# Eight weight buffers in turn for the experts of a two-layer trunk

## The reference

```python
def moe_ffn(h, router_w, router_b, w_gate, w_up, w_down):
    ...
    _, idx = lax.top_k(sel, TOP_K)              # 2 of 16 experts for each token
    ...
    for e in range(N_EXPERTS):
        he = jax.nn.silu(t @ w_gate[e]) * (t @ w_up[e])
        out = out + gates[:, e:e + 1] * (he @ w_down[e])
```

## Time and profile before

| | us |
|---|---|
| three runs, median (lowest, highest) | 1375.0 (1374.42, 1381.2) |
| profiled execution, own time | 1374.44 |
| its span | 1372.6 |
| PE busy in the span | 1196.2 (87%) |
| DVE, ACT, POOL busy | 396.4, 221.3, 132.2 |
| moved by DMA | 325.45 MB, mean 237 GB/s |
| chain that ended last: PE, DMA, DVE | 79%, 10%, 6% |

### The profile page before, as it was taken

The page is one execution under the profiler, slowest core; times in us unless marked ns, Lnnn a source line. Parts: engine busy times, 40 slices in busy tenths (PEclk is TensorE's granted clock), DMA queues, the critical chain, the costliest instruction groups (busy, mean ns, idle before and its releaser), DMA issues.

```text
span 1372.6 us, 14516 instructions
## 1 busy us (share of the span) xinstructions
PE 1196.2 (87%) x5812; PEld 656.6 (48%) x5812; DVE 396.4 (29%) x742; ACT 221.3 (16%) x414; POOL 132.2 (10%) x118
## 2 busy tenths in 40 slices
PE   4899998899999399999999099989999399999772
PEld 1444444676644245454544055646764245545440
DVE  0131114774323712121201531126532501111002
ACT  2120121112312210101010312231121210011000
POOL 0002101630000000000000201112100000000001
PEclk8899998979999599999999599999999599999997
DMA  9321115443543269999997512236256269999994
GB/s 358 152 76 61 63 61 213 186 177 131 197 171 122 93 225 401 427 403 430 400 428 270 179 62 82 102 123 234 104 233 276 105 229 397 429 426 426 428 428 177
DMA packets 34016, 325.45 MB, mean 237 GB/s; under 512 B 5664, under 2 KB 5664, under 8 KB 16288
## 3 DMA queue, kind: packets, MB, share of 16 engines
q1 hardware_dynamic: 23328, 292.03, 52.9%
q0 software_dynamic: 4896, 17.83, 3.6%
q10 hardware_dynamic: 5728, 14.68, 2.8%
HBM read 308.79 MB, written 15.74 MB: 236 GB/s over the span
## 4 chain that ended last, share of the span: by engine, by line
PE 79%; DMA 10%; DVE 6%; ACT 2%; issue 2%; POOL 1%; SPq 0%; ACTq 0%; DVEq 0%; POOLq 0%
PE ps L781 14%; PE ps L1123 13%; PE ps L1120 8%; PE ps L1150 6%; PE ps L1025 6%; PE ps L768 6%; PE ps L1145 4%; DMA arena<-in_w_down 4%; PE ps L714 3%; PE ps L938 2%; DMA ring<-in_w_mod 2%; DMA arena<-in_w_up 2%; PE ps L954 2%; PE ps L1100 2%; PE ps L982 1%
## 5 line engine op out<-in xcount | busy, mean ns | idle before, releaser
L781 PE MATMUL ps<-ring,featT 128*128 128x512 f32 (+1 forms) x480 | 186.9, 550 | 0.0
L781 PEld LDWEIGHTS ps<-ring,featT 128*128 128x128 f32 x480 | 90.8, 190 | 92.3 <-issue 89.9
L1933 DVE TENSOR_TENSOR arena<-arena,ps 128x256 f32<-128x256 f32 (+1 forms) x32 | 16.7, 522 | 284.6 <-PE ps L1123 151.1
L1123 PE MATMUL ps<-ring,arena 128*128 128x512 f32 x192 | 90.1, 627 | 2.4 <-ACT arena L1407 2.4
L1123 PE MATMUL ps<-arena 128*128 128x512 f32 x192 | 84.9, 595 | 2.4 <-ACT arena L1407 2.4
L1150 PE MATMUL ps<-arena 128*128 128x512 f32 x192 | 85.3, 597 | 0.0
L768 PE MATMUL ps<-featT,ring 128*128 128x512 f32 (+1 forms) x192 | 82.6, 589 | 2.3 <-ACT featT L1231 2.3
L1145 PE MATMUL ps<-arena 128*64 128x512 f32 x320 | 74.3, 607 | 10.9 <-DMA arena<-in_w_down 6.6
L1025 PE MATMUL ps<-ring,featT 128*128 128x512 f32 x192 | 82.7, 592 | 0.0
L1120 PE MATMUL ps<-arena 128*64 128x256 f32 x640 | 75.1, 388 | 6.3 <-DMA arena<-in_w_up 3.8
L1120 PE MATMUL ps<-ring,arena 128*64 128x256 f32 x640 | 73.4, 382 | 4.6 <-DMA ring<-in_w_gate 2.3
(11 more groups left out here) (276 smaller groups left out, 1406.4 us busy)
## 6 DMA issues: line engine op xcount, KB each, us to landing
arena<-in_w_down SPq DMA_DIRECT2D x32, 2048.0 KB, 15.0
ring<-in_w_mod SPq DMA_DIRECT2D x21, 2048.0 KB, 7.5
arena<-in_w_gate SPq DMA_DIRECT2D x16, 2048.0 KB
arena<-in_w_up SPq DMA_DIRECT2D x16, 2048.0 KB, 14.6
ring<-in_w_gate SPq DMA_DIRECT2D x16, 2048.0 KB, 12.4
ring<-in_w_up SPq DMA_DIRECT2D x16, 2048.0 KB, 13.3
ring<-in_w_in SPq DMA_DIRECT2D x10, 2048.0 KB, 8.1
ring<-in_w_out SPq DMA_DIRECT2D x4, 2048.0 KB, 8.0
```

Source lines behind the costliest of these rows:

```text
L781: o = mm(bank[:, lo:hi], featT[:, k, P * i:P * i + P], W[:, k, lo:hi], start=k == 0, stop=k == KD - 1)
L1123: o = mm(ps[:, m, :], X_[:, k, :], W[:, k, :], start=k == 0, stop=k == KD - 1)
```

## The change

There are eight buffers of 2 MB: the six from before, `tokA` (called `rows`) and `featT`. The matrices of a layer are numbered in the order in which PE uses them, gate 0, up 0, (none), gate 1, up 1, down 0, gate 2, up 2, down 1, ..., and matrix n goes to buffer n % 8, but for three of each 24. A refill waits for the product that read that buffer's last matrix.

Ahead of the experts SP issues gate 0, up 0, gate 1, up 1 when attention is done, down 0 when the output projection is done, and, once the order is known, gate 2, up 2 (behind `turn_pe`) and down 1 (behind `f_stored`). Then come the refills: the first round's first half is written out, the rest is a loop of 24 matrices for each 8 experts. The last matrix, down 15, goes to `rows` behind gate 14. PE waits on the semaphore of the buffer. DVE counts `rows_free` at a round's end, after a wait for its own last sum into `h`.

```diff
+        rows = tokA.rearrange("p t d -> p (t d)")
+        buffers = [slots[2], slots[3], rows, slots[4], slots[5], ring[:, 0, :], ring[:, 1, :], featT.rearrange("p k c -> p (k c)")]
...
+        N_TURN = 24
+        def buffer_of(n):
+            return {8: 2, 9: 0, 10: 1}.get(n % N_TURN, n % 8)
+        def load_of_weights(p, j):
+            return 3 * p + j + (3 if j == 2 else 0)
+        def position(n):
+            return n // 3 - (n % 3 == 2), n % 3
+        def last_in_buffer(n):
+            return next(m for m in range(n - 1, -N_TURN, -1) if buffer_of(m) == buffer_of(n))
+        def loads_so_far(n):
+            return sum(buffer_of(m) == buffer_of(n) and m != 2 for m in range(n + 1))
...
                 sp.wait_ge(S("na_out"), upto("na_out", l, nt))
-                load_expert(0, 0, 2)
-                for j in range(3):
-                    load_expert(1, 1, j)
+                for n in (0, 1, 3, 4):
+                    load_expert(position(n)[0], n)
                 for n in range(N_OUT):
                     name, ll, value = use_of(("out", l, n))
                     sp.wait_ge(S(name), upto(name, ll, value))
-                load_expert(0, 0, 0)
-                load_expert(0, 0, 1)
+                load_expert(0, 5)
...
-                wide_weights(1, expert_at(2), 0)
-                with sp.Fori(0, more * (NE // 2) + (NE // 2 - 2)) as i:
-                    e = [expert_at(i * 2 + 2 + n) for n in range(3)]
-                    wide_weights(i * 2 + 2, e[1], 1)
-                    down_weights(i * 2 + 1, e[0], 0)
-                    wide_weights(i * 2 + 3, e[2], 0)
-                    down_weights(i * 2 + 2, e[1], 1)
-                ...
+                def load_behind(n, place, e):
+                    p, j = position(last_in_buffer(n))
+                    if buffers[buffer_of(n)] is rows and position(n) == (1, 2) and not isinstance(place, int):
+                        sp.wait_ge(S("rows_free"), first * 2 + i)
+                    sp.wait_ge(S(("gate_pe", "up_pe", "dn_pe")[j]), first * NE + place + (p + 1))
+                    load_expert(e, n)
+                e = {p: expert_at(p) for p in range(2, 4)}
+                load_expert(e[2], 6)
+                sp.wait_ge(S("turn_pe"), upto("turn_pe", l, KD))
+                load_expert(e[2], 7)
+                sp.wait_ge(S("f_stored"), upto("f_stored", l, 16))
+                load_expert(1, 8)
+                load_behind(9, 0, e[3])
+                load_behind(10, 0, e[3])
+                load_behind(11, 0, e[2])
+                for n in range(12, N_TURN, 3):
+                    ...
+                    load_behind(n, 0, now)
+                    load_behind(n + 1, 0, now)
+                    load_behind(n + 2, 0, behind)
+                with sp.Fori(1, R * 2) as i:
+                    for n in range(0, N_TURN, 3):
+                        ...
+                        load_behind(n, i * (N_TURN // 3), now)
+                        load_behind(n + 1, i * (N_TURN // 3), now)
+                        load_behind(n + 2, i * (N_TURN // 3), behind)
+                last = expert_at(NE - 1)
+                sp.wait_ge(S("gate_pe"), first * NE + more * NE + (NE - 1))
+                load_expert(last, 2)
...
-                    pe.wait_ge(S(f"slot{3 * (q % 2) + m}"), r.all * (NE // 2 * 16) + (q // 2 + 1) * 16)
-                    return slots[3 * (q % 2) + m].rearrange("p (k c) -> p k c", k=k)
+                    n = load_of_weights(q, m)
+                    b = buffer_of(n)
+                    per_round = 6
+                    pe.wait_ge(S(f"slot{b}"), r.all * (per_round * 16) + loads_so_far(n) * 16)
+                    return buffers[b].rearrange("p (k c) -> p k c", k=k)
...
+                if l == 0:
+                    dve.sem_inc(S("rows_free"), 1)
...
                     add_rows(n_round)
+                    dve.wait_ge(S("h_end"), NT + ended(l, first, n_round, T))
+                    dve.sem_inc(S("rows_free"), 2)
```

More of the change, by code:

```diff
@@ L623, in _, with load_expert @@
                         layer_rows(l)
-                def load_expert(e, c, j):
-                    slot = 3 * c + j
-                    src = (ins["w_gate"], ins["w_up"], ins["w_down"])[j]
+                def load_expert(e, n):
+                    src = (ins["w_gate"], ins["w_up"], ins["w_down"])[n % 3]
                     w = src[l, e] if isinstance(e, int) else src[l, bass.ds(e, 1)].rearrange("o p c -> (o p) c")
-                    sp.dma_start(slots[slot], w).then_inc(S(f"slot{slot}"), 16)
+                    b = buffer_of(n)
+                    sp.dma_start(buffers[b], w).then_inc(S(f"slot{b}"), 16)
                 sp.wait_ge(S("na_out"), upto("na_out", l, nt))
-                load_expert(0, 0, 2)
-                for j in range(3):
-                    load_expert(1, 1, j)
+                for n in (0, 1, 3, 4):
+                    load_expert(position(n)[0], n)
                 for n in range(N_OUT):
@@ L667, in _ @@
-                with sp.Fori(0, more * (NE // 2) + (NE // 2 - 2)) as i:
-                    e = [expert_at(i * 2 + 2 + n) for n in range(3)]
-                    wide_weights(i * 2 + 2, e[1], 1)
-                    down_weights(i * 2 + 1, e[0], 0)
-                    wide_weights(i * 2 + 3, e[2], 0)
-                    down_weights(i * 2 + 2, e[1], 1)
-                e = [expert_at(NE - 2), expert_at(NE - 1)]
-                wide_weights(more * NE + (NE - 2), e[1], 1)
-                down_weights(more * NE + (NE - 3), e[0], 0)
@@ L676, in _ @@
-                down_weights(more * NE + (NE - 2), e[1], 1)
+                def load_behind(n, place, e):
[5 more added lines that the diff above has]
+                e = {p: expert_at(p) for p in range(2, 4)}
@@ new lines, in _ @@
+                load_expert(e[2], 6)
[7 more added lines that the diff above has]
+                for n in range(12, N_TURN, 3):
+                    p = n // 3
+                    now, behind = expert_at(p), expert_at(p - 1)
+                    load_behind(n, 0, now)
+                    load_behind(n + 1, 0, now)
+                    load_behind(n + 2, 0, behind)
@@ new lines, in _ @@
+                with sp.Fori(1, R * 2) as i:
+                    for n in range(0, N_TURN, 3):
+                        p = i * (N_TURN // 3) + n // 3
+                        now, behind = expert_at(p), expert_at(p + (NE - 1))
+                        load_behind(n, i * (N_TURN // 3), now)
[3 more added lines that the diff above has]
+                sp.wait_ge(S("gate_pe"), first * NE + more * NE + (NE - 1))
```

## The result

| | before | after |
|---|---|---|
| median of 20 runs, us | 1375.5 | 1382.3 |
| lowest, highest | 1366.7, 1392.3 | 1377.7, 1395.5 |
| profiled execution, own time | 1374.44 | 1377.88 |
| its span | 1372.6 | 1376.0 |

The changed kernel is slower: ratio 1.0081, 95% interval 1.0058 to 1.0104. The ratio (+11 us) is wider than the step between the medians (+6.8 us) and than that between the means of all twenty executions (+6.4 us, 0.47%), because it leaves out the five longest executions of the kernel before (1389 to 1392 us) and none of the changed one, of which seven are as long (1388.6 to 1395.5).

A forecast was written before the change was run, and what follows sets the result against it. It took TensorE to bound layer 0's expert part and, late in layer 1's, the weight transfers. Terms +6.0 + 6.4 - 6.8 + 0.2 = +5.8 us on 1374.44 gave 1380.2, say 1380; range 1368 to 1386.

The forecast's parts named there:

- What bounds each layer: Expert parts: TensorE sets layer 0; in layer 1 transfers take over from 1250.80 us, with a ceiling of 21.6 us to win.
- The collision: Each layer's first gather of token rows meets the three early loads and lands later: +6.0 us in layer 0, +6.4 in layer 1.
- The step that took the median of the other gathers: First gather of each layer: expected to take 10.7 us, the median over all 22 gathers, instead of 4.70 and 4.32.
- Rival A: First gathers slip in between the loads and land at 6.4 us: -2.8 us in all, 1371.6; chance 0.25.
- rival B: First gathers wait for all three loads (+8, +9), layer 1 gives back only -2.2: +15.0 us, 1389; chance 0.25.
- The gain: Layer 1's expert part: prefetch less the pauses of the new buffer order, -6.8 us, bounds -9.8 and -2.8; layer 0: 0.
- The prefetch itself: Layer 1's expert part: two matrices fewer to move while the DMA engines are full, 9.8 us less; 0 in layer 0.
- the first pause: Layer 1: up 5's refill waits for g3's end, leaving the DMA engines dry up to 3.6 us, taken as +3.0.
- The second pause: Down 9's refill waits for d7, gate 11 and up 11 queued behind it: taken as 0, up to 4 us in layer 1.
- DVE's added wait: DVE's wait for its own last row sum, once per layer, before the next layer's statistics: +0.1 to +0.3 us, taken as 0.2.
- the step from the sum to the call: From +5.8 us and a 0.5% bound of 6.9 us to chances: faster 0.15, within 0.5% 0.52, slower 0.33.

The follow-up runs named there:

- e6: The e2 kernel, but in layer 0 the three extra matrices wait until gate product 0 is done: 1370.2 us, ratio 0.9989 to the kernel before.
- e3: The changed kernel with its eight buffers in plain first-in-first-out order: 1380.1 us, ratio 1.0042 to the kernel before.
- e7: The changed kernel timed again without an edit: 1379.5 us, ratio 1.0058 to the kernel before.
- e1: The changed kernel with gate 2, up 2 and down 1 issued only after the layer's first gather has landed: 1368.8 us, ratio 0.9953 to the kernel before.
- e2: The changed kernel with down 1 issued before the order is known, gate 2 with it, up 2 behind the first gather: 1367.0 us, ratio 0.9937 to the kernel before.
- e5: The changed kernel with the edits of e2 and e3 together: 1368.0 us, ratio 0.9959 to the kernel before.

## Why the prediction was right or wrong

Its time, 1380, lies between the profiled execution and the median, and its range holds both. Its call was wrong: it put 0.52 on a change within 0.5% and 0.33 on slower, and the ratio says slower.

**What bounds each layer: right.** Layer 0's 256.66 us don't move in any of the kernels, with five, six or eight matrices ahead (e6, before, after). In layer 1 the distance follows the transfers.

**The collision: right in place, cause and size.** Forecast +6.0 and +6.4, measured +6.6 and +6.3 from issue to landing. The step that took the median of the other gathers for the row to go by held. Rival A, in which the gather slips in between, is out. The rule on turns between queues (the Trainium skill, "DMA: Bandwidth & Descriptors", section "Queues, rings and completion order") isn't contradicted: the gather landed at 481.7, 2.3 us before the third matrix, which was issued at 465.96 and took 18.0. These runs don't show how long one turn is. (The +8 of rival B for layer 0 was worked out too high: by the prediction's own numbers the end of the three loads is +7.3.)

**The gain: mis-sized.** Forecast -6.8, measured 235.62 - 227.14 = 8.5. The prefetch itself is right: e3 gets 9.85 of the two matrices' 9.8. The term that was off is the first pause, set at 3.0: e3 says 1.4. The working had the engines without work for up to 3.6 us there. They weren't: in the 12 us around it (1166 to 1178 us) they are busy to 0.99 and move 374 GB/s, where the kernel before moves 411 (1154 to 1166). The missing 0.44 MB are 1.0 us. The second pause, set at 0, costs nothing that can be seen, by the rates given at e3.

**The rest.** DVE's added wait was set at 0.2: the next layer's statistics start 1.39 us behind the start of the last sum, where it was 1.15. The first two products of layer 1 took 15.56 us instead of 17.04. That is the clock's rise at the start of the experts, not the change: it is 15.4 to 17.1 over all runs, 17.06 in e7 of the same kernel, and the granted clock of the first 4 us is 0.60 here and 0.50 in e1, where the two take 16.95. Without this the profiled pair would differ by some 4.9 us, near the forecast's 5.8.

**What failed is the step from the sum to the call.** The prediction took 0.5%, 6.9 us, for "about what a measurement of this kernel tells from no change", and with a sum of +5.8, 1 us under that bound, it put 0.52 inside and only 0.33 on slower. The measurement is finer than that: its interval is 0.23% to either side, 3 us, and 0.40% in e7, and both lie wholly above 1. So a change of the forecast's own size shows as slower.

The second lack is a term for executions that differ by 12 us and more from one to the next. The profiled pair says +3.4, the sum of the measured terms 12.8 - 8.5 = +4.3, the medians +6.8 and, in e7, +5.9; the ratios 1.0081 and 1.0058, with e3 at 1.0042, between them +5.8 and +11. Of the changed kernel 8 in 20 runs and 4 in 12 had a mean clock of 0.925 or less and took 1384 to 1396 us; of the kernel before 5 in 35 and 2 in 29, and 5 of the first 20 took 1389 to 1392 us (their clocks are not on record). With all of these left out on both sides the medians are 1380.8 against 1374.4, +6.3, and in e7 1378.4 against 1373.1, +5.3: the forecast's 5.8 lies between. These are 0.46% and 0.39%; so the runs settle that the change is slower, but not on which side of 0.5% it lies. The change itself costs some 5 to 6 us, and why the 1.0081 lies above that stands with the result. Of these 5 to 6 us the measured terms hold 4.3; for the rest no trace shows a place.

Whether the change makes the long executions more frequent is not shown. The counts lean that way, 26 of 92 executions of the kernels with eight buffers against 13 of 96 of those with six, but they are uneven (e2 has none in 12, e5 has 5), and one trace of such an execution puts 12 of its 17 us where the change has no instruction. It stays open.

Rival B was right that the change is slower, but not in its mechanism: the gathers landed before the three loads had ended, and layer 1 gave back 8.5 us, not 2.2.

## What to carry to other kernels

Engines that idle don't make a prefetch free, if a small transfer that someone waits for comes right behind it: look for the next transfer on the critical path, and hold the large ones until it has landed. Here one wait turned +6 us into -6 us. A stretch bounded by TensorE gains nothing from earlier weights, and the collision is paid in both layers. Where the forecast lies beside a bound, the chances should be near even on both sides of it, not 0.52 to 0.33. And the rates of two kernels are compared over the same piece of work: in the kernel before, 1136 to 1176 us gives 404 GB/s and 1138 to 1178 gives 416.

## What the runs showed of the hardware that was not expected

The same instructions took 12 us more in one stretch of one execution, with the clock at 0.50 from about 1000 to 1034 us while TensorE was busy; in the other execution the same fall lasted under 10 us. What decides this no run shows. And the last down product of each layer, which starts after a short idle stretch, takes 3.68 us in some executions and 5.38 in others (1350.70 above, at a granted clock of 1.00, 1340.68 in e1, at 0.68) with the same shapes. The distances between fixed products, on the other hand, repeat to 0.3 us across the traces (226.97 to 227.23 for the changed order of buffers in eight of them): they tell 1.4 us apart where twelve timed runs did not.
